# A decoder step on one core: weight split in chunks, turned head order, and the last norm moved into the experts' block

## The reference

```
proj = x @ w_in                                  # [u | q | k | v]
a = differential attention (causal, ALiBi), RMS norm per head
s = S5 scan of u, GELU, GLU
x = layer_norm(ALPHA * x + concat(a, s) @ w_out)
gates = route(x)                                 # 1 of 4 groups, then top 2 of its 4 experts
for e in range(16):
    h = silu(x @ w_gate[e]) * (x @ w_up[e])      # 1024 -> 512
    out = out + gates[:, e:e+1] * (h @ w_down[e])
x = layer_norm(ALPHA * x + out)
```

## Time and profile before

| | us |
|---|---|
| time of the kernel, median of 3 | 1235.85 (1231.47 to 1237.33) |
| the profiled execution: its time | 1233.69 |
| its span, first to last instruction | 1231.9 |
| PE busy | 1060.7 (86%) |
| DVE busy | 689.7 (56%) |
| ACT busy | 514.7 (42%) |
| POOL busy | 328.9 (27%) |

### The profile page before, as it was taken

The page is one execution under the profiler, slowest core; times in us unless marked ns, Lnnn a source line. Parts: engine busy times, 40 slices in busy tenths (PEclk is TensorE's granted clock), DMA queues, the critical chain, the costliest instruction groups (busy, mean ns, idle before and its releaser), DMA issues. The chain is left out here.

```text
span 1231.9 us, 17307 instructions
## 1 busy us (share of the span) xinstructions
PE 1060.7 (86%) x5508; PEld 869.0 (71%) x5509; DVE 689.7 (56%) x1279; ACT 514.7 (42%) x736; POOL 328.9 (27%) x567
## 2 busy tenths in 40 slices
PE   6998998998699999999961679999999999999610
PEld 5886788897466686688841568888888887888500
DVE  3555547240688724475548464446566689576327
ACT  4241321323477644422110344444555677465213
POOL 0715354800500000000000123333433452435316
PEclk9997999899699999999985689999999999999865
DMA  7130240203740062723310746667769799888243
GB/s 235 44 102 18 65 128 31 64 1 96 276 148 1 2 194 93 285 103 127 121 57 0 270 173 186 225 241 270 246 212 322 257 345 388 275 306 269 54 159 149
DMA packets 51249, 201.33 MB, mean 163 GB/s; under 512 B 9107, under 2 KB 15635, under 8 KB 45043
## 3 DMA queue, kind: packets, MB, share of 16 engines
q1 hardware_dynamic: 40674, 138.43, 31.7%
q0 software_dynamic: 7488, 27.27, 9.1%
q10 hardware_dynamic: 3024, 34.87, 7.3%
HBM read 163.81 MB, written 36.73 MB: 163 GB/s over the span
## 5 line engine op out<-in xcount | busy, mean ns | idle before, releaser
L2046 DVE TENSOR_TENSOR wlo<-raw,whi 128x4096 fp32r<-128x4096 f32 x48 | 211.5, 4423 | 94.3 <-ACT whi L1975 94.1
L1975 ACT ACTIVATE whi<-raw 128x4096 fp32r<-128x4096 f32 x48 | 175.0, 3649 | 91.6 <-SPq L1848 38.7
L1884 POOL DMA_INDIRECT acc<-eyb,idxs x25 | 67.4, 2695 | 149.6 <-ACT eyb L1993 149.6
L1917 PE MATMUL psY<-whi,ehs 128*128 128x512 f32 x200 | 82.1, 410 | 10.1 <-DVE wlo L2046 10.1
L1917 PE MATMUL psG<-whi,exs 128*128 128x512 f32 x200 | 83.1, 415 | 4.1 <-DVE exs L2051 3.9
L1918 PE MATMUL psG<-wlo,exs 128*128 128x512 f32 x200 | 80.7, 403 | 0.0
L1919 PE MATMUL psG<-whi,exs 128*128 128x512 f32 x200 | 80.5, 403 | 0.0
L1918 PE MATMUL psY<-wlo,ehs 128*128 128x512 f32 x200 | 79.7, 398 | 0.0
L1919 PE MATMUL psY<-whi,ehs 128*128 128x512 f32 x200 | 79.6, 398 | 0.0
L1917 PE MATMUL psU<-whi,exs 128*128 128x512 f32 x200 | 79.3, 397 | 0.0
L1919 PE MATMUL psU<-whi,exs 128*128 128x512 f32 x200 | 79.2, 396 | 0.0
(11 more groups left out here) (390 smaller groups left out, 2451.1 us busy)
## 6 DMA issues: line engine op xcount, KB each, us to landing
raw<-in_moe_w_gate SPq DMA_DIRECT2D x16, 2048.0 KB, 8.8
raw<-in_moe_w_up SPq DMA_DIRECT2D x16, 2048.0 KB, 9.7
raw<-in_moe_w_down ACTq DMA_DIRECT2D x16, 2048.0 KB, 8.3
w_raw<-in_w_in SPq DMA_DIRECT2D x27, 256.0 KB, 3.5
stg<-in_x_prompt SPq DMA_DIRECT2D x8, 512.0 KB, 4.1
kc<-in_cache_k SPq DMA_DIRECT2D x16, 256.0 KB, 3.0
vc<-in_cache_v SPq DMA_DIRECT2D x16, 256.0 KB, 3.0
mr<-in_w_out SPq DMA_DIRECT2D x8, 512.0 KB, 3.2
```

Source lines behind the costliest of these rows:

```text
L1884: nc.gpsimd.indirect_dma_start(s.acc, bass.IndirectOffsetOnAxis(ap=idxs[:, 0:1], axis=0), yb[j][:, :], None, compute_op=ALU.add).then_inc( ...
L1917: pe.matmul(out, hi, w_hi, start=(k == 0), stop=False)
L1975: nc.scalar.activation(whi[:, at], s.raw[:, at], ACT.Copy).then_inc(hi_made[i], 1)
L2046: nc.vector.tensor_tensor(wlo[:, at], s.raw[:, at], whi[:, at].bitcast(F32), ALU.subtract) \
```

## The change

It has three parts. First, every second head goes through its query blocks from the widest to the narrowest. Second, ScalarE's copy and VectorE's subtraction of a weight piece are cut into four chunks each, the semaphores count chunks, and TensorE waits within a product for the chunk that it needs next. The loads still wait for whole pieces; `split_by` is therefore multiplied by 4. Third, the last norm is moved into the block of the experts, without a barrier ahead of it: SyncE loads the rows into `raw` once all scatters have landed and the weight loads are in. VectorE measures blocks 0, 1 and 8, ScalarE blocks 2 to 7 by two accumulating passes. Roots are taken in five groups. VectorE normalises in place with two fused operations, and GpSimd has no part in it. The removed function `combine` is left out here, as are lines that only rename.

```
-    steps = [(h, i) for h in range(H) for i in range(QB)]
+    steps = [(h, i) for h in range(H) for i in (range(QB) if h % 2 == 0 else range(QB - 1, -1, -1))]
...
-                ch(ts(s.split_by[:, :], count[0:1, 0:E], ne[:, 0:1], w0[:, 0:1], ALU.add, ALU.min))
+                ch(ts(eb[:, 0:E], count[0:1, 0:E], ne[:, 0:1], w0[:, 0:1], ALU.add, ALU.min))
+                ch(ts(s.split_by[:, :], eb[:, 0:E], 4.0, None, ALU.mult))
...
+TOGETHER = ((0,), (1,), (2, 3), (4, 5), (6, 7, 8))
+ACT_STATS = (2, 3, 4, 5, 6, 7)
...
+        z = [s.raw[:, b * D:(b + 1) * D] for b in range(NBLK)]
...
+        def quarter(i, c):
+            a, n = PIECES[i][0], (PIECES[i][1] - PIECES[i][0]) // 4
+            return slice(a + n * c, a + n * (c + 1))
...  SyncE, after its loads
+                sp.wait_ge(loads_in, 1)
+                sp.wait_ge(all_added, 1)
+                for b in range(NBLK):
+                    r = rows(b)
+                    sp.dma_start(z[b][0:r, :], s.acc[b * P:b * P + r, :]).then_inc(z_in[b], 16)
+                for b in range(NBLK):
+                    sp.wait_ge(biased, b + 1)
+                    sp.dma_start(dst, z[b][0:r, :]).then_inc(o_out, 16)
+                sp.wait_ge(o_out, 16 * NBLK)
...  GpSimd, after the last scatter has landed
+                pool.sem_inc(all_added, 1)
...  TensorE
+                def product(out, x, steps, at, wait_for=None):
                     for k in range(steps):
+                        if wait_for is not None and k % (steps // 4) == 0:
+                            wait_for(k // (steps // 4))
...
+                    done = 4 * entry(pe, 1, b, 1, E) + 1
...
+                    product(psG[:, :], xs[j], KD, lambda k: GATE_AT + k * FE,
+                            lambda c: pe.wait_ge(lo_made[0], done + c)).then_inc(g_made, 1)
...  the same for up, and for the first half of down
...  ScalarE
-                    at = slice(*PIECES[i])
-                    nc.scalar.activation(whi[:, at], s.raw[:, at], ACT.Copy).then_inc(hi_made[i], 1)
+                    for c in range(4):
+                        at = quarter(i, c)
+                        nc.scalar.activation(whi[:, at], s.raw[:, at], ACT.Copy).then_inc(hi_made[i], 1)
...
-                act.sem_inc(all_sent, 1)
-                act.wait_ge(all_sent, 1)
+                act.sem_inc(loads_in, 1)
+                nc.scalar.activation(warm[:, :], gcol[:, :], ACT.Sqrt)
+                def act_stats(b):
+                    act.wait_ge(z_in[b], 16)
+                    junk = yb[1][:, :]
+                    n = ACT_STATS.index(b) + 1
+                    if n > 1:
+                        act.wait_ge(act_var, n - 1)
+                    nc.scalar.activation(junk, z[b][:, :], ACT.Copy, scale=-1.0 / (32 * D), accum_out=part[:, b:b + 1]) \
+                        .then_inc(mean_made, 1)
+                    act.wait_ge(mean_made, n)
+                    nc.scalar.activation(junk, z[b][:, :], ACT.Square, scale=1.0 / 32, bias=part[:, b:b + 1],
+                                         accum_out=var[:, b:b + 1]).then_inc(act_var, 1)
+                for g, some in enumerate(TOGETHER):
+                    for b in some:
+                        if b in ACT_STATS:
+                            act_stats(b)
+                    at = slice(some[0], some[-1] + 1)
+                    act.wait_ge(var_ready, g + 1)
+                    nc.scalar.activation(var[:, at], var[:, at], ACT.Sqrt).then_inc(rooted, 1)
...  VectorE
-                    at = slice(*PIECES[i])
-                    dve.wait_ge(hi_made[i], entry(dve, 1, b, 1, E))
-                    nc.vector.tensor_tensor(wlo[:, at], s.raw[:, at], whi[:, at].bitcast(F32), ALU.subtract) \
-                        .then_inc(lo_made[i], 1)
+                    before = 4 * entry(dve, 1, b, 1, E)
+                    for c in range(4):
+                        at = quarter(i, c)
+                        dve.wait_ge(hi_made[i], before + c + 1)
+                        nc.vector.tensor_tensor(wlo[:, at], s.raw[:, at], whi[:, at].bitcast(F32), ALU.subtract) \
+                            .then_inc(lo_made[i], 1)
...
+                def stats(b):    # bn_stats of two halves, bn_aggr
+                def guard(g):    # waits for act_var; var += EPS / ALPHA ** 2; mean = part * -32
+                def turn_root(g):    # waits for rooted; rstd = 1 / var
+                def normalise(b):
+                    zb = z[b][0:r, :]
+                    nc.vector.scalar_tensor_tensor(zb, zb, mean[0:r, b:b + 1], s.lg2[0:r, :], ALU.subtract, ALU.mult).then_inc(weighted, 1)
+                    dve.wait_ge(weighted, b + 1)
+                    nc.vector.scalar_tensor_tensor(zb, zb, rstd[0:r, b:b + 1], s.lb2[0:r, :], ALU.mult, ALU.add).then_inc(biased, 1)
+                stats(0)
+                guard(0)
+                stats(1)
+                turn_root(0)
+                guard(1)
+                normalise(0)
+                turn_root(1)
+                normalise(1)
+                for g in range(2, len(TOGETHER)):
+                    if g == len(TOGETHER) - 1:
+                        stats(QB)
+                    guard(g)
+                    turn_root(g)
+                    for b in TOGETHER[g]:
+                        normalise(b)
```

More of the change, by code:

```diff
@@ L138, in scores @@
                 nk = (i + 1) * P
-                if i == 0:
+                if n % QB == 0:
                     pe.wait_ge(q_kept[h], 1)
@@ L1819, in experts @@
         w_in = [sem(f"ex_w{i}") for i in range(3)]
+        z = [s.raw[:, b * D:(b + 1) * D] for b in range(NBLK)]
+        cst, mv = sb("cst", [P, 2, 6]), sb("cmv", [P, NBLK, 5])
+        warm = sb("warm", [P, 1])
+        mean, var, rstd, part = (mv[:, :, k] for k in range(4))
+        all_added, loads_in, cseq, mean_made, act_var, var_ready, rooted, weighted, biased, o_out = (
+            sem("co_" + n) for n in "all_added loads_in seq mean act_var var rooted weighted biased o_out".split())
+        z_in = [sem(f"co_z{b}") for b in range(NBLK)]
         def over_blocks(eng, block):
@@ L1909, in turn_x @@
                     last.then_inc(x_turned, 1)
-                def product(out, x, steps, at):
+                def product(out, x, steps, at, wait_for=None):
                     for k in range(steps):
+                        if wait_for is not None and k % (steps // 4) == 0:
+                            wait_for(k // (steps // 4))
                         hi, lo = (part[:, k * P:(k + 1) * P] for part in x)
@@ L1941, in down @@
                 def down(b, j):
-                    count = entry(pe, 1, b, 1, E) + 1
-                    pe.wait_ge(lo_made[2], count)
+                    done = 4 * entry(pe, 1, b, 1, E) + 1
                     pe.wait_ge(h_split, b + 1)
@@ L1997, in load_down @@
                     act.dma_start(s.raw[:, slice(*PIECES[2])], expert_weights(io, e, 2)).then_inc(w_in[2], 16)
+                for i in range(3):
+                    act.sem_inc(hi_made[i], 4)
                 high(0, 0)
@@ new lines, in _ @@
+                ch = Chain(dve, cseq)
+                ch(nc.vector.memset(mv[:, QB, :], 1.0))
+                def stats(b):
+                    r = rows(b)
+                    dve.wait_ge(z_in[b], 16)
+                    nc.vector.bn_stats(cst[0:r, 0, :], z[b][0:r, 0:512])
+                    ch(nc.vector.bn_stats(cst[0:r, 1, :], z[b][0:r, 512:D]))
+                    ch(nc.vector.bn_aggr(mv[0:r, b, 0:2], cst[0:r, :, :].rearrange("p a b -> p (a b)")))
+                def guard(g):
+                    some = TOGETHER[g]
+                    at = slice(some[0], some[-1] + 1)
+                    mine = [b for b in some if b in ACT_STATS]
+                    if mine:
+                        dve.wait_ge(act_var, ACT_STATS.index(mine[-1]) + 1)
+                    nc.vector.tensor_scalar(var[:, at], var[:, at], EPS / ALPHA ** 2, None, ALU.add).then_inc(var_ready, 1)
+                    if mine:
+                        of = slice(mine[0], mine[-1] + 1)
+                        ch(nc.vector.tensor_scalar(mean[:, of], part[:, of], -32.0, None, ALU.mult))
@@ new lines, in turn_root @@
+                def turn_root(g):
+                    some = TOGETHER[g]
+                    at = slice(some[0], some[-1] + 1)
+                    dve.wait_ge(rooted, g + 1)
+                    ch(nc.vector.reciprocal(rstd[:, at], var[:, at]))
+                def normalise(b):
+                    r = rows(b)
+                    zb = z[b][0:r, :]
+                    nc.vector.scalar_tensor_tensor(zb, zb, mean[0:r, b:b + 1], s.lg2[0:r, :], ALU.subtract, ALU.mult)                         .then_inc(weighted, 1)
+                    dve.wait_ge(weighted, b + 1)
+                    nc.vector.scalar_tensor_tensor(zb, zb, rstd[0:r, b:b + 1], s.lb2[0:r, :], ALU.mult, ALU.add)                         .then_inc(biased, 1)
```

78 lines of the change are left out of this document (10 added, 68 removed).

## The result

| | before | after |
|---|---|---|
| median, us | 1233.66 (1230.84 to 1237.33, 4 runs) | 1199.97 (1196.51 to 1208.41, 4 runs) |
| ratio | | 0.9728, 95% interval 0.9695 to 0.9761 |
| the profiled execution: its time | 1233.69 | 1196.51 |
| its span | 1231.9 | 1194.7 |
| PE busy | 1060.7 | 1048.9 (88%) |

The change takes 33.7 us off the median, 37.2 between the two profiled spans. Two executions that stand far apart, one of 2140 us in `late_sub` and one of 2710 us in the runs of before beside it, are left out of the ratios.

A forecast was written before the change was run, and what follows sets the result against it. TensorE was taken to bound the experts' middle (417.9 of 430 us), so gains lay where it waits or has ended. Terms -8.0 - 2.1 - 5.9 + 0.5 - 5.4 - 4.7 = -25.6 gave 1210.3 us, range 1201 to 1220.

The forecast's parts named there:

- What the chunks cost: Experts' stage: longer VectorE and ScalarE work per piece lies hidden beside busy TensorE, and new waits cost nothing; +0.5 us.
- Attention, turned order: Attention stage: shorter waits at head changes and a shorter final drain; -8.0 us, ends -3.4 and -11.7.
- First block: First expert block: VectorE's split of the down weights ends sooner by starting one chunk behind ScalarE's copy; -2.1 us.
- Last block: Last expert block: TensorE starts its down product on the first chunks instead of whole pieces; -5.9 us.
- Drain and barriers: After the last scatter: the norm's loads go out ahead of GpSimd's drain and the barrier; -5.4 us.
- The norm: First landing to last store's issue: fused VectorE passes, with ScalarE measuring blocks 2 to 7; 31.0 against 35.66, -4.7 us.
- The start: Unchanged code ahead of the attention: no difference forecast, 0.
- (1): Attention: the head-change waits only move, so it gives 3.4 instead of 8.0 us; 1214.9 us, chance 0.10.
- (2): Norm: ScalarE switches tables between Square and Sqrt, adding six loads, 6.3 us; 1216.6 us, chance 0.08.
- (3): Experts' products: the new waits break TensorE's stream, costing 0.16 x 225 = 36 us; 1246 us, chance 0.04.
- (4): First and last expert blocks: chunks bring nothing, through a later load and low clock; 1215.4 us, chance 0.05.

The follow-up runs named there:

- late_sub: The changed kernel, but VectorE starts a piece's four subtractions only when all four of ScalarE's copies are made; 1210.74 us, ratio 0.9792 to before.
- whole_waits: The changed kernel, but TensorE waits for a piece's fourth chunk at the start of each product, with no waits in mid-product; 1205.23 us, ratio 0.9757 to before.
- norm_stage: The changed kernel with the norm's new arithmetic in a stage of its own behind the old stage border; 1206.89 us, ratio 0.9786 to before.
- turned: The kernel before with only the changed order of query blocks; 1223.71 us, ratio 0.9908 to before.
- chunks: The kernel before with only the four chunks a piece and their waits; 1224.37 us, ratio 0.9910 to before.

## Why the prediction was wrong, point by point

The direction held, and so did the mechanisms for the head changes, the splits of the first and the last block, the border and the norm; the sum was short by 8 us of 34. Two steps make this up. In **What the chunks cost** the mechanism was wrong: I held that nothing that only frees VectorE can pay in the middle of the experts' stage and added +0.5, and the runs showed -3.4. In **Attention, turned order** the mechanism held and the term was too small, -8.0 where the runs showed some -11.7: it had nothing for a clock that falls behind the stops that the new order removes. The second measurement of the changed kernel, 1204.23, lies inside my range, but its own gain of 30.4 is above my 25.6 too.

- **What the chunks cost, +0.5: -3.4.** I took the earlier trace rows to mean that nothing that frees VectorE could pay, because TensorE was busy for 417.88 of 430 us. Of the 12 us left 9.70 are the stop in the last block, which I had in a term of its own, and in the 23 blocks TensorE counts as busy for 418.67 of 421.30 us. The busy time hid what was to be had: in blocks with a new expert each, TensorE started five products late, behind the chain of load, copy and subtraction. I named the term "all loads still wait for whole pieces", and missed that the whole piece is ready sooner: VectorE's last chunk ends 6.18 us after the copy began (1137.62 to 1143.80), against 8.07 (1158.98 to 1167.05). The period of the blocks had shown it: four of 23 blocks of before lasted 18.8 to 19.6 us instead of 18.17. `late_sub` shows the cause, `whole_waits` excludes the other. In the other three executions with the old split the blocks took up to 424.14, so the gain is 3.4 to 6.2. The cost itself I had too high, 22 and 45 us, as I added up durations: 192 chunks of 1218 ns are 4.87 us a piece instead of 4.42, 192 copies of 1048 ns 4.19 instead of 3.65. But the records of chunks in a row overlap, and in busy time VectorE's 48 pieces took 221.4 us instead of 211.5 and ScalarE's 187.1 instead of 175.0.
- **Attention, -8.0: -8.9 in the profiles, -11.6 to -11.9 as a rule.** My steps gave -8.7 and I shaded that to -8.0 for narrow steps that wait on each other; in the trace TensorE's waits between narrow steps are at most 0.25 us, with 0.65 ahead of the last turn. Of the terms, waits went from 8.3 to 2.0 us (I had -8.3 and +3.0), and the drain gave 4.0 (I had 4.3). The other 2.7 to 3.0 us could not be had from the profile of before: that execution alone ran all three head changes and the drain at the higher clock. That -11.7 was also the far end of my range for this term is luck; it stood there for waits that all vanish, and 2.0 us of them are left.
- **First block, -2.1: -1.8** in its two segments, which differ by up to 2 us between executions of the same code. From ScalarE's first copy to the second `ehs` the four executions with whole pieces take 52.6 to 53.4 us, and the six with chunks, their waits and the old place of the load 49.9 to 52.6, on average 2.2 less: right. VectorE's last chunk ends 5.73 us after the copy began (690.71 to 696.44), against 8.10; forecast 6.0. The stop is 4.47 instead of 6.23 us.
- **Last block, -5.9: -5.0.** TensorE starts 2.83 us after the copy began, forecast 2.3, as VectorE's first chunk starts 1.55 and not 1.14 us after ScalarE's. The last comes at 10.19, forecast 9.5, since the clock did fall for seven matmuls, 1.4 us, though waiting for chunks would have cost a part of it anyway.
- **Drain and barriers, -5.4: -5.5.** Right; `norm_stage` gives it back (+5.7).
- **The norm, -4.7: -5.6.** A block's two passes take 1.31 + 1.20 = 2.51 us, not 2 x 1.29: 22.6 instead of 23.2. The small operations of five groups are 2.7 instead of 3.0, the statistics 4.7 instead of 4.8.
- **The start, 0: -7.3.** Unchanged code ahead of the attention. The event came at 317.42 us in before's profile and between 309.53 and 316.09 in the thirteen others, 312.5 on average, in copies of both kernels alike. That is the execution, not the change. It hid that the attention of the same execution was fast, so that its time agreed with the median.

With these sizes, each from few executions, the sum is -11.7 - 1.8 - 3.4 - 5.0 - 5.5 - 0.3 - 5.6 + 0.6 = -32.7, between the 33.7 and the 30.4 that were measured.

The rivals: (1), head-change waits only move, falls (2.0 left of 8.3, `turned` gives 11.4). (2), table switches, falls: one load ahead of six pairs of Copy and Square with five Sqrt between them. (3), the broken stream, falls at 0.00 us a wait. (4), chunks bring nothing, falls (`chunks` gives 11.1). My range ended at 1201: its low end held the attention at its best and small gains in the first block and the norm, and no gain in the longest stretch.

Where I cited the Trainium skill, VectorE: DVE Perf Modes, section "The TRN2 errata — SBUF-src ops pay a fixed extra latency per instruction", a fixed cost for each instruction is what the durations show: 4.87 against 4.42 us a piece for three more instructions, 0.15 each. In VectorE's busy time it is 0.07 each. That one large tile pays it once and many small ones pay it each is true here and does not decide the time, since the piece is a link in a chain of two engines.

## What to carry to other kernels

Where one engine's result is another's input and a buffer is freed at the end, cutting the work into chunks shortens the chain even as each instruction's sum grows; price it as first chunk plus the slower engine's whole, and look for who waits on the buffer. A stretch in which the bound engine is busy for 97 to 99% still needs its period looked at block by block: the even blocks say what is possible, the uneven ones what is to be had. One profile is one execution: a stop of 1.5 to 2.2 us in TensorE's stream left the clock high in the one shown and cost 1.3 to 1.6 us behind it in others, so a stop removed can be worth more than its own length. Put a few executions of each kernel side by side, stretch by stretch, before a difference of 2 us is read.

## What the runs showed of the hardware

- The same stop and the same code behind it ran at either level of TensorE's clock in different executions: turn and product behind a stop of 1.49 us took 2.3 us at 1.00 and 4.0 at about 0.62 mean, behind 2.19 us 2.3 and 3.8 to 3.9. Of 20 such stops in five executions of the old order 8 had the lower level behind them.
- Square, Copy and Sqrt alternate without a further table load. The only one is of 1.28 us. The Trainium skill, ScalarE: Activation LUTs, section "Table sets: the hidden batching unit", names relu, copy, identity and abs as members of every set; in this trace Square needs no switch beside Sqrt either.
- Two fused passes of 1024 columns in place, the second reading what the first wrote and with a semaphore between them, start 1.31 us apart, and the next block's follows after 1.20.
- Waits that are met already, nine more in each of 23 blocks of TensorE's stream, cost nothing that the traces show: 417.92 us with them and without.
- A 2 MB load put 7.5 us sooner on ScalarE's queue, 0.8 us behind the first gather on GpSimd's, made that gather land 12.1 us after its issue instead of 5.5. Of the transfers at the start of this stage the one that the chain needs first was better off without it.
